# Two transformer blocks on one core: query projection by token tiles, and four steps of three engines placed ahead of weight splits

## The reference

```python
# block 1
h = rms_norm(x, norm1_g); proj = h @ w_in
(rx, rgate, q, kc, vc, ks, vs, kw, vw, nsa_g, mg_rnn, mg_attn) = split(proj)
hr = rg_lru(causal_dwconv(rx, rnn_conv_w, rnn_conv_b), ...)    # a, u from two gates, scan over tokens
y_rnn = (hr * gelu(rgate)) @ w_rnn_out                          # d_rnn = 1344
# nsa: 16 heads of 64, 4 K/V heads; qh = rms_norm(q per head, q_norm_g)
o = gate0 * attn(qh, compressed k, v) + gate1 * attn(qh, k_slc, v_slc) + gate2 * attn(qh, k_win, v_win)
x = x + (sigmoid(mg_rnn) * y_rnn + sigmoid(mg_attn) * (o @ w_attn_out)) @ w_out
up = causal_dwconv(rms_norm(x, norm2_g) @ w_up, ...); gate, val = split(up)
x = x + (gelu(gate) * val) @ w_down
# block 2: attention and gated mlp side by side, layer norms, silu feed-forward
```

## Time and profile before

| | us |
|---|---|
| median of 3 runs | 847.89 |
| the three runs | 847.89, 847.55, 851.02 |
| the profiled execution, its own time | 849.21 |
| its span | 847.5 |
| PE busy | 831.2 |
| DVE busy | 574.6 |
| ACT busy | 491.2 |
| POOL busy | 28.8 |

### The profile page before, as it was taken

How to read it: one execution, slowest core, us unless ns; L and a number is a source line. 1 busy time by engine, 2 the same in 40 slices (tenths; PEclk the granted TensorE clock), 3 DMA queues, 4 the chain that set the end, 5 groups by cost and what they waited for, 6 DMA issues and landing times.

```text
span 847.5 us, 12652 instructions
## 1 busy us (share of the span) xinstructions
PE 831.2 (98%) x5195; PEld 729.7 (86%) x5195; DVE 574.6 (68%) x761; ACT 491.2 (58%) x734; POOL 28.8 (3%) x40
## 2 busy tenths in 40 slices
PE   9999998999999899999999999999999999999996
PEld 8999987888888898888888888788788888888885
DVE  6572496778675766688787788767777665564555
ACT  6553387778685544476665666545854654554541
POOL 0100200000000000000000000002110000000000
PEclk9999999899999999999999999999999999999998
DMA  8436332233232467355545455376345465556441
GB/s 321 161 131 229 149 129 89 101 113 112 101 127 90 167 250 290 109 176 199 194 174 209 168 199 199 125 297 205 142 149 200 149 208 190 178 178 234 155 150 50
DMA packets 22361, 144.03 MB, mean 170 GB/s; under 512 B 2592, under 2 KB 3104, under 8 KB 7968
## 3 DMA queue, kind: packets, MB, share of 16 engines
q1 hardware_dynamic: 20880, 137.92, 45.6%
q10 hardware_dynamic: 1424, 5.31, 1.6%
HBM read 142.17 MB, written 1.05 MB: 169 GB/s over the span
## 4 chain that ended last, share of the span: by engine, by line
PE 87%; DVE 6%; ACT 3%; issue 2%; DMA 1%; POOL 0%; DVEq 0%; POOLq 0%; ACTq 0%
PE PS L1622 17%; PE PS L1625 9%; PE PS L1672 9%; PE PS L1673 9%; PE PS L1674 9%; PE PS L1612 7%; PE PS L1614 6%; PE PS L1613 6%; DVE WL L989 2%; PE PS L1711 2%; PE PS L1767 2%; PE PS L1744 1%; DVE CG L1414 1%; DMA RAW<-in_w_stream 1%; PE PS L1637 1%
## 5 line engine op out<-in xcount | busy, mean ns | idle before, releaser
L989 DVE TENSOR_TENSOR WL<-RAW,WH 128x2048 fp32r<-128x2048 f32 (+2 forms) x128 | 285.4, 2230 | 69.0 <-ACT WH L601 69.0
L601 ACT ACTIVATE WH<-RAW 128x2048 fp32r<-128x2048 f32 (+2 forms) x128 | 238.5, 1867 | 64.2 <-DMA RAW<-in_w_stream 40.5
L1612 PE MATMUL PS<-BHL,WH 128*128 128x256 f32 (+2 forms) x408 | 116.0, 284 | 0.0
L1614 PE MATMUL PS<-BHL,WL 128*128 128x256 f32 (+2 forms) x408 | 115.0, 282 | 0.0
L1613 PE MATMUL PS<-BHL,WH 128*128 128x256 f32 (+2 forms) x408 | 114.9, 282 | 0.0
L1403 DVE TENSOR_TENSOR HLS<-PS,HLS 128x512 f32<-128x512 f32 x46 | 31.7, 689 | 96.6 <-ACT HLS L896 96.6
L1622 PE MATMUL PS<-CHL,WH 128*128 128x512 f32 x368 | 92.5, 393 | 0.1
L1622 PE MATMUL PS<-BHL,WH 128*128 128x512 f32 x336 | 84.0, 392 | 0.0
L896 ACT ACTIVATE HLS<-PS 128x512 f32<-128x512 f32 x46 | 27.5, 598 | 95.7 <-PE PS L1625 91.5
L1612 PEld LDWEIGHTS PS<-BHL,WH 128*128 128x128 f32 (+2 forms) x408 | 76.7, 188 | 1.6 <-issue 1.2
L1622 PEld LDWEIGHTS PS<-CHL,WH 128*128 128x128 f32 x368 | 66.5, 188 | 13.3 <-DVE WL L989 0.6
(11 more groups left out here) (295 smaller groups left out, 1417.0 us busy)
## 6 DMA issues: line engine op xcount, KB each, us to landing
RAW<-in_w_stream SPq DMA_DIRECT2D x108, 1024.0 KB, 4.8
RAW<-in_w_stream SPq DMA_DIRECT2D x11, 1008.0 KB, 5.1
RAW<-in_w_stream SPq DMA_DIRECT2D x8, 704.0 KB, 4.1
WF<-in_w_stream SPq DMA_DIRECT2D x2, 1024.0 KB, 5.7
LN<-in_ln ACTq DMA_DIRECT2D x2, 1024.0 KB, 5.7
WF<-in_w_stream SPq DMA_DIRECT2D x4, 294.0 KB, 3.0
X<-in_x SPq DMA_DIRECT2D x2, 512.0 KB, 4.1
RAW<-in_w_stream SPq DMA_DIRECT2D x2, 512.0 KB, 7.0
```

Of the source, the lines that this page charges most:

```text
L601: eng.activation(WH[:, c % NSLOT, 0:CHUNKS[c][2]], raw(c), ACT.Copy).then_inc(w_hi, 1)
L989: eng.tensor_tensor(WL[:, c % NSLOT, 0:CHUNKS[c][2]], raw(c), f32(WH[:, c % NSLOT, 0:CHUNKS[c][2]]), ALU.subtract).then_inc(w_lo, 1)
L1612: eng.matmul(out, wh, H[0:parts, k, :], start=(k == 0), stop=False)
L1614: last = eng.matmul(out, wl, H[0:parts, k, :], start=False, stop=(k == nk - 1))
```

## The change

- `q` by token tiles: each pair of `q` chunks is two `t_half` calls into two banks of 512 columns (banks 6 and 7, then 0 and 1). ScalarE squares a token tile (512 columns), VectorE sums the squares by head (two reductions a pair), GpSimd makes rq in four powers of 8 columns, VectorE multiplies PSUM by rq into QN, TensorE transposes QN (8 of 128 by 128 a pair: the first pair behind `q` 2, the second behind `w1` 1), and ScalarE copies them to QT (`q_copy`). QT is normalised, so `unit_max`, `unit_exp` and the compressed softmax lose their rq step.
- K's copy (KT) at `cmp` 1 stands ahead of the chain of small steps.
- `rnn` 3's split stands ahead of the compressed softmax's exponential on ScalarE, and ahead of the wait for it on VectorE.
- At `ri` 1 the first gate tile is evicted before the unit's exponential.
- The last group's squares, input, scan, `rg_first` and `rg_second` stand ahead of the chunk's split, and the last two one chunk earlier.
- `up_second(23)` stands behind the split of `dn` 11, and tile 0 of `dn` 11 starts with the passes that need no WL.

```diff
--- before
+++ after
+SPLIT_IN_SOFTMAX = W0 + 3
...
-MB_READERS = {"cmp": ("act", 1), "q": ("act", 1), "rnn": ("dve", 1), "mg": ("act", 1), "ri": ("act", RG),
+MB_READERS = {"cmp": ("act", 1), "rnn": ("dve", 1), "mg": ("act", 1), "ri": ("act", RG),
...
+        Q_BANKS = (6, 0)
+        QT_BANKS = (2, 6)
...
-            eng.wait_ge(qss_copied, 1)
-            power(rq[:, :], qss[:, :], NT * NH, 1.0, HD * EPS, rq_ready)
+            for n in range(2):
+                for t in range(NT):
+                    eng.wait_ge(q_ss, NT * n + t + 1)
+                    h = slice(NH * t + 8 * n, NH * t + 8 * n + 8)
+                    power(rq[:, h], qss[:, h], 8, 1.0, HD * EPS, rq_ready)
...
-                    h = NH * qt + 4 * g + r
...
-                                          scale=rq[:, h:h + 1], accum_out=rs[:, 4 * (u % 2) + r:4 * (u % 2) + r + 1])
+                                          accum_out=rs[:, 4 * (u % 2) + r:4 * (u % 2) + r + 1])
...
-                if kind == "q":
-                    bank = wait_mb(eng, c)
-                    eng.activation(QT[:, 2 * i:2 * i + 2, :].rearrange("p k t -> p (k t)"), PS[:, bank, :], ACT.Copy)
-                    if i:
-                        eng.wait_ge(qss_done, i)
-                    eng.activation(QSQ[:, :, :].rearrange("p k t -> p (k t)"), PS[:, bank, :], ACT.Square)\
-                       .then_inc(mb_act, 1)
+                if kind == "q" and i % 2:
+                    n = i // 2
+                    if n == 1:
+                        q_copy(0)
+                    for t in range(NT):
+                        wait_tile(eng, c, t)
+                        if n == 1:
+                            eng.wait_ge(q_ss, t + 1)
+                        eng.activation(QSQ[:, t, :], PS[:, Q_BANKS[n] + t, :], ACT.Square).then_inc(q_sq, 1)
...
+                if kind == "rnn" and i == 0:
+                    q_copy(1)
...
-                    if 0 <= c - W0 - U0 < NU:
-                        unit_exp(c - W0 - U0)
                     for m, t in enumerate(gate_order(i)):
+                        if m == RG_TILES[i] - 2 and 0 <= c - W0 - U0 < NU:
+                            unit_exp(c - W0 - U0)
...
+            def q_copy(n):
+                eng.wait_ge(qkt_done, n + 1)
+                b = QT_BANKS[n]
+                eng.activation(QT[:, 4 * n:4 * n + 4, :], PS[:, b:b + 2, :].rearrange("p b (k t) -> p (b k) t", k=2), ACT.Copy)\
+                   .then_inc(qkt_copied, 1)
...
+                if rg_group(c - W0, RG_INPUT) == NG - 1:
+                    rg_first(NG - 1)
                 if CHUNKS[c][:2] not in SUMS_FIRST and CHUNKS[c][0] != "ri":
                     split(c + 2)
-                if rg_group(c - W0, RG_SCAN) == NG - 1:
-                    rg_first(NG - 1)
                 if c - W0 == 3:
...
                 if c - W0 == 3:
+                    split(c + 2)
...
-                if CHUNKS[c][0] == "ri":
+                if CHUNKS[c][0] == "ri" and c != SPLIT_IN_SOFTMAX:
...
-                m = mx[:, 4 * (u % 2):4 * (u % 2) + 4]
-                link(eng.tensor_reduce(m.rearrange("p (b r) -> p b r", b=2), s_view(2, qt), AX, ALU.max, negate=True))
-                q = heads4(rq[:, NH * qt:NH * qt + NH], 4 * g)
-                if u == 0:
-                    eng.wait_ge(rq_ready, 1)
-                eng.tensor_tensor(nb[:, 4 * (u % 2):4 * (u % 2) + 4].rearrange("p (b r) -> p b r", b=2),
-                                  m.rearrange("p (b r) -> p b r", b=2), q, ALU.mult).then_inc(nb_ready, 1)
+                m = nb[:, 4 * (u % 2):4 * (u % 2) + 4]
+                eng.tensor_reduce(m.rearrange("p (b r) -> p b r", b=2), s_view(2, qt), AX, ALU.max, negate=True)\
+                   .then_inc(nb_ready, 1)
...
-                        link(eng.tensor_tensor(SC[:, tt, :, :], SC[:, tt, :, :], per_head(cmx, tt), ALU.subtract))
-                        ins = eng.tensor_tensor(SC[:, tt, :, :], SC[:, tt, :, :], per_head(rq, tt), ALU.mult)
+                        ins = eng.tensor_tensor(SC[:, tt, :, :], SC[:, tt, :, :], per_head(cmx, tt), ALU.subtract)
...
+                    split(W0 + w + 2)
...
+                if kind == "cmp":
+                    eng.wait_ge(kt_done, i + 1)
+                    eng.wait_ge(gk_ready, 1)
+                    bank = (2, 6)[i]
+                    eng.tensor_scalar(KT[:, i, :, :], PS[:, bank:bank + 2, :].rearrange("p b (g t) -> p (b g) t", g=2),
+                                      gk[:, 1 + i:2 + i], None, ALU.mult).then_inc(kt_copied, 1)
...
-                if kind == "w1" and i == 1:
-                    eng.wait_ge(qss_done, 4)
-                    eng.tensor_copy(qss[:, :], PS[:, 5, 0:NT * NH]).then_inc(qss_copied, 1)
+                if kind == "q" and i % 2:
+                    n = i // 2
+                    heads = "p (h d) -> p h d"
+                    for t in range(NT):
+                        h = slice(NH * t + 8 * n, NH * t + 8 * n + 8)
+                        eng.wait_ge(q_sq, NT * n + t + 1)
+                        eng.tensor_reduce(qss[:, h], QSQ[:, t, :].rearrange(heads, h=8), AX, ALU.add).then_inc(q_ss, 1)
+                    for t in range(NT):
+                        h = slice(NH * t + 8 * n, NH * t + 8 * n + 8)
+                        eng.wait_ge(rq_ready, NT * n + t + 1)
+                        eng.tensor_tensor(QN[:, n, t, :].rearrange(heads, h=8), PS[:, Q_BANKS[n] + t, :].rearrange(heads, h=8),
+                                          rq[:, h].unsqueeze(2).broadcast_to([P, 8, HD]), ALU.mult).then_inc(kn_ready, 1)
...
-                if c and CHUNKS[c - 1][0] == "ri":
+                if c and CHUNKS[c - 1][0] == "ri" and c - 1 != SPLIT_IN_SOFTMAX:
...
-                    up_second(N_UP - 1)
                 if kind == "up2":
                     halves_sum(N_UP + i, UP2_BANKS[i % 2])
+                if rg_group(c - W0, RG_SQUARES) == NG - 1:
+                    rg_squares(NG - 1)
+                if rg_group(c - W0, RG_INPUT) == NG - 1:
+                    rg_input(NG - 1)
+                    rg_scan(NG - 1)
+                    rg_second(NG - 1)
                 if CHUNKS[c][:2] not in SUMS_FIRST and kind != "ri":
                     split(c + 2)
+                if CHUNKS[c - 1][:2] == ("up", N_UP - 1):
+                    up_second(N_UP - 1)
                 G = rg_group(c - W0, RG_SQUARES)
-                if G is not None:
+                if G is not None and G < NG - 1:
                     rg_squares(G)
                 G = rg_group(c - W0, RG_INPUT)
-                if G is not None:
+                if G is not None and G < NG - 1:
                     rg_input(G)
-                    if G == NG - 1:
-                        rg_scan(G)
                 G = rg_group(c - W0, RG_SCAN)
-                if G is not None:
-                    (rg_second if G == NG - 1 else rg_scan)(G)
+                if G is not None and G < NG - 1:
+                    rg_scan(G)
                 side(c)
                 if kind == "ri" and i:
...
+                    if m < 4:
+                        eng.wait_ge(kn_ready, 4 * NT)
...
-                    eng.wait_ge(kt_copied, 2)
+                    eng.wait_ge(qkt_copied, 2)
...
-                    bank = mb_bank(MB_NO[c])
-                    for j in range(2):
-                        last = f_tile(PS[:, bank, 256 * j:256 * j + 256], c, 1024 * j, P, BH, BL)
+                    b = Q_BANKS[i // 2]
+                    if i == 0:
+                        eng.wait_ge(kt_copied, 2)
+                    if i == 2:
+                        eng.wait_ge(mb_act, 2)
+                    last = t_half(c, (b, b + 1), i, BH, BL)
...
+                        eng.wait_ge(w_hi, SPLIT_NO[c + 1] + 1)
+                        eng.wait_ge(lo_s, 2 * i + 3)
+                        eng.wait_ge(up_hi if kind == "dn" else up2_hi, 2 * i + 4)
+                        s = (c + 1) % NSLOT
+                        outs = [PS[:, first_bank + n, :] for n in range(2)]
+                        units = [(2 * i + 2 + k) % NA for k in range(2)]
+                        def weights(W, k, n):
+                            return W[:, s, 1024 * k + 512 * n:1024 * k + 512 * n + 512]
+                        for n in range(2):
+                            eng.matmul(outs[n], AH[:, units[0], 0:P], weights(WH, 0, n), start=False, stop=False)
+                            eng.matmul(outs[n], AL[:, units[0], 0:P], weights(WH, 0, n), start=False, stop=False)
+                            eng.matmul(outs[n], AH[:, units[1], 0:P], weights(WH, 1, n), start=False, stop=False)
                         eng.wait_ge(w_lo, SPLIT_NO[c + 1] + 1)
+                        for n in range(2):
+                            eng.matmul(outs[n], AH[:, units[0], 0:P], weights(WL, 0, n), start=False, stop=False)
+                            eng.matmul(outs[n], AH[:, units[1], 0:P], weights(WL, 1, n), start=False, stop=False)
                         eng.wait_ge(lo_s, 2 * i + 4)
```

(37 more changed lines are left out.)

17 lines of the change are left out of this document (4 added, 13 removed).

## The result

The changed kernel takes 838.47 us (median of 838.43, 841.08, 838.19 and 838.52), the kernel before beside it 847.81; the ratio is 0.9888, with a 95% interval of 0.9857 to 0.9919. The forecast was 837.5. The profiled execution took 838.43, with a span of 836.7; before it was 849.21 and 847.5. The medians are 9.3 us apart and the two profiled executions 10.8, because the one profiled before was itself 1.3 above its median.

A forecast was written before the change was run, and what follows sets the result against it. TensorE, busy 98% of the span, was taken to bound the kernel. Terms of -3.2, +2.1, -1.1, -2.0, -3.3, -3.0 and -1.2 sum to -11.7, from 849.2 to 837.5 us; range 834.8 to 842.0.

The forecast's parts named there:

- q's work: In q, wider matmuls and fewer head sums, less added transposes, save TensorE 3.2 us.
- The wait on QN: Ahead of q's first transposes, TensorE waits for normalised tiles: 2.1 us added, bounds 1.2 and 3.2.
- Compressed softmax to unit 3: Up to unit 3's scores, an earlier WL lands the next chunk sooner: -1.1 us, bounds 0 and -2.5.
- `ri` 1: At ri 1, evicting the gate tile first removes TensorE's wait for its bank: -2.0 us.
- the low clock: Behind ri 1, the half-rate stretch goes if its window is not half idle: -3.3 us, bounds 0 and -3.3.
- The first low stretch: The clock's fall at 105.70, following 32 matmuls of 32 columns, was expected to stay.
- Last group: Ahead of ro 0, moving steps before the splits removes the whole wait for AL: -3.0 us, bounds -2.0 and -3.1.
- `dn` 11: At dn 11, the wait of 1.4 for WL goes, leaving some wait for x: -1.2 us, bounds -0.8 and -1.5.
- the wait in q: A rival had the new wait in q lower the clock, costing 1.7 us: 839.2, chance 0.30.
- the second rival: ScalarE holds the attention stage, so gains there and behind come to nothing: about 841.6, chance 0.13.
- The full clock at 105: One alternative within a rival: ri 0 runs at full clock, 2 us less, 835.4; that rival's chance 0.10.
- the third rival: No wait in q, or no low clock at 105: 2 us less, 835.4, chance 0.10.

The follow-up runs named there:

- no_softmax: The changed kernel with the split in the compressed softmax back at its old place; 839.41 us, ratio 0.9882 to the kernel before.
- no_ri: The changed kernel with the unit's exponentials ahead of the gate tiles' evictions at ri 1 again; 841.43 us, ratio 0.9893 to the kernel before.
- q_alone: The changed kernel with its four other moves undone, keeping q by token tiles and K's earlier copy; 845.36 us, ratio 0.9956 to the kernel before.
- no_last: The changed kernel with the last group's steps behind the splits again on both engines; 843.98 us, ratio 0.9923 to the kernel before.
- after: The changed kernel itself, in its first profiled execution, set against the kernel before; 838.43 us, span 836.7.

## Why the prediction was right, point by point

*q's work, -3.2.* Too much by 0.5: the chunks came at 0.230 to 0.235 us a matmul, not 0.227, so four took 22.2 us instead of 21.8, and the second transposes took 1.0, not 0.8. The Trainium skill (TensorE: Matmul & The Clock Gate, Back-to-back issue gap) gives N/2.4 + 2.5 ns as the gap of a single matmul, 0.216 us for these, and says that a stream of pairs of weight load and matmul measured about 0.131 us at 512 columns. No stretch of q here comes down to either, and the trace decides.

*The wait on QN, +2.1.* Too much by 0.6. On the changed kernel's VectorE and GpSimd:

```profile
59.28 2.29 DVE L1006 TENSOR_TENSOR WL<-RAW,WH 128x2048 fp32r<-128x2048 f32 x1 [0.72 <-ACT WH L608]
61.49 1.27 DVE L1225 TENSOR_REDUCE qss<-QSQ 128x8 f32<-128x512 f32 x2
...
66.21 0.69 DVE L1229 TENSOR_TENSOR QN<-PS,rq 128x512 f32<-128x512 f32 x1 [1.31 <-POOL rq L549]
```

The chain is the one told: split, sums of 0.68, two powers in a row, the last product at 66.9 (forecast 67.2), with TensorE there at 65.3 (64.9). The two errors, 0.5 and 0.6, cancel, which is luck; q nets -1.11, forecast -1.1.

*Compressed softmax to unit 3, -1.1.* The stage from `w1` to unit 1's scores gave 2.0, and the cause was another. The step that failed is that the gain comes of WL ("it ends about 6.5 us earlier and the chunk lands at about 114, before ScalarE wants it"): the chunk did land in time, and `no_softmax` shows that nothing hung on it once the two products and the scale were gone. I had named the two products as gone, in brackets, and priced only the landing; I had not seen that each exponential's scale goes too. The wait ahead of unit 3 stayed at 0.6 in starts (0.4 by the list).

*`ri` 1, -2.0, and the low clock, -3.3.* In this pair of profiles 1.8 (first to third gate tile, 3.83 us before and 2.02 after) and 3.1 (from there to the mask, 7.42 and 4.30). As causes they were priced wrong. q's form alone takes the wait from 1.9 to 1.4 by the list, so the move itself is worth 1.2 (`no_ri`), and no clock was seen to hang on it: `no_ri` and `q_alone` wait 1.4 there and keep the full clock, while the two profiles of the kernel before wait 1.9 and fall, for 6.8 and 3.4 us. Whether a wait of 1.9 would bring the fall in the changed kernel, no run shows. At `ro` 0 waits of 3.0 to 3.3 were followed by a fall in two profiles of four. In the executions together a difference stays: of 37 more executions of the kernel before none was granted over 0.995 on average, of the changed kernel's ten 7 had 0.997 or more. The first low stretch, which I left in, was absent in both profiles of the changed kernel, and present in six of its ten variants.

*Last group, -3.0:* measured -3.12, and `no_last` +3.2. The bound of the working does not hold together: it has AL at 291.2 at the latest and WL of `ro` 0, which stands behind AL, at 290.0. In `after` AL ended at 279.93 and that WL at 282.15, 1.4 ahead of `ro` 0's start. *`dn` 11, -1.2:* measured -1.16 and 1.1, with 0.5 in starts (0.3 by the list) of wait for X in place of WL, where I gave 0.4.

*What I did not see:* +1.3 in the second block. No term had room for it, and it happens to offset what the attention stage gave beyond its forecast. By stages the misses are -0.9 up to unit 1, +0.3 at `ri` 1, -0.1 at `ro` 0, +0.4 between there and the up stage, and +1.3: the sum of -11.7 missed the profiled -10.8 by 0.9.

*The rivals.* No low stretch follows the wait in q in any profile; the next one comes 36 us later or more. ScalarE does hold the stage up to unit 3 in the kernel before, but the change lightens ScalarE there, which the second rival left out. The full clock at 105, half of the third rival, came true, and 835.4 did not: that stretch had cost nothing before. That a low stretch ends as soon as full matmuls come is not what the trace of before shows: the first ended at 109.06, and the first full ones start at 110.69.

## What to carry to other kernels

Before you price an edit by where it moves work, list what its new form takes out of every later chain (here a product, a scale, a factor); that was worth more than the move beside it. Price a low clock as a chance, from several executions, and ask what other engine would have been waited for there anyway. When a wait turns up far from the edit, look which load in flight changed neighbours, that of the program's own instructions among them.
